# Seven half-size products for the first matrix of each MLP as well, in a float32 decoder trunk on one Trainium2 core

## The chip, the core and the metric

The kernel runs on one NeuronCore of a Trainium2 chip. The core has a matrix engine (TensorE, called PE below; its loads of stationary operands are listed apart as PEld), a vector engine (VectorE, DVE), a scalar engine (ScalarE, ACT), a general engine (GpSimd, POOL), and SyncE (SP), which here only starts transfers. Sixteen DMA engines move data between HBM and the on-chip memory SBUF; matrix products land in PSUM, which has eight banks of 512 float32 per partition. Each engine works through its own list of instructions in order and waits on semaphores that other engines raise.

The metric is the device time of one execution in microseconds (us), lower being better.

## What is computed

The input is 512 tokens of width 1024. A recurrent layer (Griffin RG-LRU) is followed by an MLP, then a differential-attention layer and a second MLP, and a final norm. The change touches the two MLPs and what lies around them:

```
def sq_relu_mlp(h, w1, w2):
    u = jax.nn.relu(h @ w1)
    return (u * u) @ w2

x = x + sq_relu_mlp(rmsnorm(x, mlp_norm[l]), mlp_w1[l], mlp_w2[l])   # for each of the two layers
```

`w1` is 1024 x 4096, `w2` is 4096 x 1024, and everything is float32. The kernel keeps float32 accuracy by writing each operand as hi + lo (hi is the operand rounded to the format fp32r, lo the rest) and adding three products: hi with hi, hi with lo, lo with hi.

## The kernel before, in words

All weights stream through the core as tiles of 128 x 1024 (512 KB). For every tile SP starts a load into one of two buffers (`w_raw`), ACT writes the rounded copy (`split_hi`, into one of four slots `w_hi`), DVE writes the rest (`split_lo`, into `w_lo`), and PE multiplies with both. ACT may write tile t's slot only when PE has finished tile t - 4 (the semaphore `tile_done`), so splits run at most three tiles ahead of PE.

Each MLP is cut into four groups of 1024 hidden columns. A group has two halves.

The first product ("up", `mlp_up`): eight tiles of `w1`, each 24 matmuls of 512 columns (8 chunks of the input x three products), all 512 tokens at once, results in banks 0 to 3. After each tile ACT takes the relu from PSUM and squares it, and ACT and DVE write the hi and lo parts of the activations.

The second product ("down", `mlp_down`) uses Winograd's form of Strassen's method over halves of the tokens, of the hidden columns and of the outputs: seven products of half size instead of eight. Its operands are sums of quarters. The activations' sums are made by DVE (`pair_sums`). The weights' sums are made in transit: POOL starts a DMA that adds a tile from HBM to what lies in a buffer (`accum_op=ALU.add` into `b11` or `b12`; "an add" below). An add may start when the split of the buffer's former content is done. A group has 14 tiles here, each 12 matmuls of 512 columns, 8 adds, 4 loads into `b11` and `b12` and 12 loads into `w_raw`. DVE adds the finished products to `y` (`add_product`), and PE waits for that (`y_read`) two products later.

The order of the work on every engine is written out by hand: the functions `mlp_up` and `mlp_down` stand once under each engine, each with its own order, and an engine that waits holds up all that stands behind it.

The new code has one function `mlp` on ACT and on DVE that counts tiles s = 0 to 27 of a group (0 to 13 up, 14 to 27 down). In the text that follows tile s means this count.

## Time and profile before

| | |
|---|---|
| median of 3 runs | 1066.42 us (1066.36 to 1066.42) |
| the profiled execution, and its span | 1066.65 us, 1065.0 us |
| PE busy | 1051.8 us, 99% of the span |
| DVE busy | 697.8 us, 66% |
| ACT busy | 583.0 us, 55% |
| POOL busy | 91.3 us, 9% |
| moved by DMA | 136.80 MB, 128 GB/s on average |
| the eight MLP groups | 81.6 us each |

A row of a group of instructions names the line, the engine, what is written and read, the shapes and the count, then busy time and the mean of one in ns, then the idle time of the engine just before them and what ended it. "PE 99%" does not say that PE works at its peak: the ends of matmuls are modelled, and consecutive ones overlap in the records. The distance from start to start tells the pace.

### The profile page before, as it was taken

The page shows a single profiled execution, that of the slowest core. Times are in us where ns is not written, and L with a number is a line of the kernel's source. Part 1 is how long each engine was busy: PE and PEld are TensorE (multiplying, and loading weights), DVE is VectorE, ACT ScalarE, POOL GpSimd, SP SyncE. Part 2 cuts the span into 40 slices and gives each one's busy share as a digit, 9 for nine tenths or more (in the row PEclk, how much of TensorE's full clock was granted, in tenths as well). Part 3 has the DMA queues.
Part 4 walks back from the last instruction along what each step waited for, and adds up shares of the span by engine and source line. Part 5 has one row for each costly group of instructions (what it writes and reads, how often), then busy time and mean ns, then how long its engine had stood idle before and what let it go on. Part 6 is the DMA issues. An engine that isn't in the chain of part 4 may idle for free.

```text
span 1065.0 us, 12738 instructions
## 1 busy us (share of the span) xinstructions
PE 1051.8 (99%) x4752; PEld 848.1 (80%) x4752; DVE 697.8 (66%) x1149; ACT 583.0 (55%) x948; POOL 91.3 (9%) x105
## 2 busy tenths in 40 slices
PE   9999999999999999999999999999999999999996
PEld 6777888888888888888877777778888888888884
DVE  7888865665665575579656666565475675565666
ACT  6699845536535535545435656555543643643654
POOL 1000041100100100100000000031100010010012
PEclk9999999999999999999999999999999999999998
DMA  7222237665665575542311111136467468367372
GB/s 263 80 79 93 80 125 198 103 210 157 103 195 163 102 194 179 99 119 89 130 60 60 60 61 40 60 104 193 99 134 224 115 122 238 101 136 231 105 158 79
DMA packets 38940, 136.80 MB, mean 128 GB/s; under 512 B 4448, under 2 KB 4576, under 8 KB 38752
## 3 DMA queue, kind: packets, MB, share of 16 engines
q1 hardware_dynamic: 29232, 101.20, 28.1%
q0 software_dynamic: 9216, 33.56, 18.8%
q10 hardware_dynamic: 432, 1.24, 0.3%
q8 instruction: 38, 0.62, 0.2%
q14 instruction: 22, 0.18, 0.1%
HBM read 133.89 MB, written 2.10 MB: 128 GB/s over the span
## 4 chain that ended last, share of the span: by engine, by line
PE 95%; DVE 2%; DMA 1%; ACT 1%; issue 0%; SPq 0%; DVEq 0%; ACTq 0%
PE ps L1646 55%; PE ps L1774 28%; PE ps L1832 4%; PE ps L1891 2%; PE ps L1917 2%; PE ps L1700 1%; PE ps L1906 1%; DMA x<-x_t 0%; DVE w_lo L996 0%; DVE acc L1025 0%; DMA w_raw<-weights 0%; PE ps L1758 0%; PE ps L1929 0%; PE ps L1766 0%; DVE value L1344 0%
## 5 line engine op out<-in xcount | busy, mean ns | idle before, releaser
L1646 PE MATMUL ps<-h_hi,w_hi 128*128 128x512 f32 x704 | 281.7, 400 | 1.0 <-DVE w_lo L1014 0.6
L1646 PE MATMUL ps<-h_hi,w_lo 128*128 128x512 f32 x704 | 275.1, 391 | 0.0
L1646 PE MATMUL ps<-h_lo,w_hi 128*128 128x512 f32 x704 | 274.9, 391 | 0.0
L538 ACT ACTIVATE w_hi<-w_raw 128x1024 fp32r<-128x1024 f32 x150 | 158.6, 1057 | 192.1 <-DMA w_raw<-weights 92.0
L996 DVE TENSOR_TENSOR w_lo<-w_raw,w_hi 128x1024 fp32r<-128x1024 f32 x150 | 183.8, 1238 | 56.8 <-ACT w_hi L538 56.4
L1774 PE MATMUL ps<-w_hi,a_hi 128*128 128x512 f32 x448 | 174.4, 389 | 0.0
L1774 PE MATMUL ps<-w_lo,a_hi 128*128 128x512 f32 x448 | 174.3, 389 | 0.0
L1774 PE MATMUL ps<-w_hi,a_lo 128*128 128x512 f32 x448 | 174.3, 389 | 0.0
L1646 PEld LDWEIGHTS ps<-h_hi,w_hi 128*128 128x128 f32 x704 | 132.6, 188 | 32.8 <-DVE w_lo L1014 3.0
L1646 PEld LDWEIGHTS ps<-h_lo,w_hi 128*128 128x128 f32 x704 | 132.9, 189 | 28.0 <-issue 1.9
L1646 PEld LDWEIGHTS ps<-h_hi,w_lo 128*128 128x128 f32 x704 | 132.6, 188 | 28.2
L802 ACT ACTIVATE w_hi<-b 128x1024 fp32r<-128x1024 f32 x80 | 84.4, 1056 | 90.7 <-PE ps L1774 53.9
L1312 DVE TENSOR_TENSOR w_lo<-b,w_hi 128x1024 fp32r<-128x1024 f32 x80 | 97.7, 1238 | 41.6 <-ACT w_hi L802 41.6
L1344 DVE SCALAR_TENSOR_TENSOR value<-ps,scale,value 128x512 f32<-128x512 f32 x104 | 73.4, 747 | 63.1 <-PE ps L1774 63.0
L502 POOL DMA_DIRECT2D b<-weights x64 | 54.8, 857 | 541.2 <-DVE w_lo L1312 371.3
L1774 PEld LDWEIGHTS ps<-w_lo,a_hi 128*128 128x128 f32 x448 | 84.1, 188 | 17.6
L1774 PEld LDWEIGHTS ps<-w_hi,a_hi 128*128 128x128 f32 x448 | 84.1, 188 | 17.5 <-DVE w_lo L1312 0.2
L1774 PEld LDWEIGHTS ps<-w_hi,a_lo 128*128 128x128 f32 x448 | 84.1, 188 | 17.3
L760 ACT ACTIVATE work<-ps 128x512 f32<-128x512 f32 x64 | 37.9, 593 | 86.1 <-PE ps L1646 86.0
L1285 DVE TENSOR_TENSOR a_lo<-work,a_hi 128x256 fp32r<-128x256 f32 x64 | 35.5, 555 | 39.4 <-ACT a_hi L769 39.3
L1646 PE MATMUL ps<-u_hi,w_hi 128*128 128x512 f32 x128 | 51.7, 404 | 0.0
L1646 PE MATMUL ps<-u_hi,w_lo 128*128 128x512 f32 x128 | 50.0, 391 | 0.0
(179 smaller groups left out, 1234.6 us busy)
## 6 DMA issues: line engine op xcount, KB each, us to landing
w_raw<-weights SPq DMA_DIRECT2D x150, 512.0 KB, 3.5
b<-weights POOLq DMA_DIRECT2D x64, 512.0 KB, 5.4
b<-weights SPq DMA_DIRECT2D x32, 512.0 KB, 5.7
x<-x_t SPq DMA_DIRECT2D x8, 256.0 KB, 6.2
y_t<-value SPq DMA_DIRECT2D x8, 256.0 KB, 2.3
w_raw<-weights SPq DMA_DIRECT2D x4, 256.0 KB, 5.1
gw<-gate_weights ACTq DMA_DIRECT2D x1, 1024.0 KB, 6.0
gain_rows<-final_gain SPq DMA_DIRECT2D x1, 512.0 KB, 6.5
```

What stands on the lines that cost most here:

```text
L502: nc.gpsimd.dma_start(to[:, half, :], weights[stored_tile(layer, g, place + half)], accum_op=ALU.add).then_inc(sum_in[name][half], 16)
L538: nc.scalar.activation(w_hi[:, t % RING, :], w_raw[:, r % RAWS, :], ACT.Copy).then_inc(whi_done, 1)
L760: nc.scalar.activation(work[:, m % 2, :], ps[:, m % RING, :], ACT.Relu).then_inc(bank_read, 1)
L802: nc.scalar.activation(w_hi[:, t % RING, :], QUARTERS[q][:, half, :], ACT.Copy).then_inc(whi_done, 1)
L996: nc.vector.tensor_tensor(w_lo[:, t % RING, :], w_raw[:, r % RAWS, :], w_hi[:, t % RING, :], ALU.subtract).then_inc(wlo_done, 1)
L1285: nc.vector.tensor_tensor(a_lo[:, j, first:end, :].rearrange("p o s -> p (o s)"), src, a_hi[:, j, first:end, :].rearrange("p o s -> p (o s)"),
L1312: nc.vector.tensor_tensor(w_lo[:, t % RING, :], QUARTERS[q][:, p % 2, :], w_hi[:, t % RING, :], ALU.subtract).then_inc(wlo_done, 1)
L1344: return nc.vector.scalar_tensor_tensor(out=to, in0=bank, scalar=scale2[:, half, tok:tok + 1], in1=to, op0=ALU.mult, op1=ALU.add)
L1646: ins = nc.tensor.matmul(ps[:, bank, :], w[:, slot, ws], o[:, k, :], start=(k == 0 and n == 0), stop=(k == NCH - 1 and n == 2))
L1774: ins = nc.tensor.matmul(ps[:, bank, :], a[:, j, op, ts], w[:, slot, ws], start=first and a is a_hi and w is w_hi, stop=end and w is w_lo, ...
L1832: ins = nc.tensor.matmul(ps[:, 4 * half + tok, :], o[:, k, ts], w[:, t % RING, cs], start=(i == 0 and n == 0), stop=(i == NCH - 1 and n == 2))
L1891: ins = nc.tensor.matmul(ps[:, BANK_SCORES + 2 * (j % 2) + c, 0:n], kq[rows, h % 2, 1, qb * P:(qb + 1) * P], kq[rows, h % 2, 0, 0:n], star ...
```

## The change

The first product of each MLP group is computed with seven products of halves as well, over halves of the input width, of the hidden columns and of the tokens. Its 14 tiles have 24 matmuls of 256 columns each. The operands made from x are prepared once per layer as halves and sums (`x_hi`, `x_lo`, seven of them), in `residual_step`. The weights' sums of both products come through two pairs of buffers, `q1` and `q2`, by a list (`SOURCES`) that says, per product, which buffer is read after how many loads and adds; `None` is a tile straight from `w_raw`. The three partial results that several outputs share are copied out of PSUM by ACT (`copied`) and added by DVE (`up_sum`). The activations' operands (`a_hi`, `a_lo`) now live in four slots and are made one product ahead of their use instead of all before the down product. The on-chip memory is laid out as one region with different tenants by stage.

```diff
+UP = ((H11, 0, True), (T1, 1, True), (T2, 0, False), (H21, 2, True), (T3, 0, False), (H22, 1, False),
+      (T4, 0, False))
...
-PER = NCH + 2 * NPROD
+PER = 4 * NPROD
...
+SOURCES = (("q2", 0, 0), ("q1", 0, 1), ("q1", 0, 2), None, ("q2", 0, 1), ("q1", 0, 3), None,
+           ("q1", 1, 3), ("q1", 1, 4), ("q1", 1, 5), None, ("q2", 1, 2), None, ("q1", 1, 6))
...
+            def load_group(layer, g):
...
+                load_quarter(layer, g, "q2", A11, down_tile(layer, g - 1, 8) if g else None)
+                if g:
+                    two(r, A12)
+                    load_quarter(layer, g, "q1", A21, down_tile(layer, g - 1, 12))
...
+            def add_first(layer, g):
+                add_quarter(layer, g, "q1", A22, loaded=0)
+
+            def add_others(layer, g):
+                for n in ((2, 0) if g == 0 else (0, 2)):
+                    if n:
+                        add_quarter(layer, g, "q1", A11, split=up_tile(layer, g, 2))
+                    else:
+                        add_quarter(layer, g, "q2", A21, split=up_tile(layer, g, 0))
+                add_quarter(layer, g, "q1", A12, split=up_tile(layer, g, 4))
+                add_quarter(layer, g, "q2", B22, loaded=1)
+                add_quarter(layer, g, "q1", B12, split=down_tile(layer, g, 0))
+                add_quarter(layer, g, "q1", B22, split=down_tile(layer, g, 2))
+                add_quarter(layer, g, "q1", B21, split=down_tile(layer, g, 4))
...
+            add_first(1, 0)
             accumulate(N_M1)
...
+            add_others(1, 0)
```

On ACT (`activated(…, 3)` reads banks 0 and 1, where the last up product ends):

```diff
+            def activated(layer, g, n):
+                group = layer * GROUPS + g
+                src, to, sign = ((r11[:, :], r11[:, :], 1.0), (r22[:, :], r22[:, :], -1.0),
+                                 (r12[:, :], r12[:, :], 1.0), (up_banks(0), r21, -1.0))[n]
+                if n < 3:
+                    act.wait_ge(up_added, 3 * group + n + 1)
+                else:
+                    act.wait_ge(tile_done, down_tile(layer, g, 0))
...
+                ins = nc.scalar.activation(to, src, ACT.Relu, scale=sign).then_inc(relu_done, 1)
+                act.wait_ge(relu_done, 4 * group + n + 1)
+                nc.scalar.activation(to, to, ACT.Square).then_inc(squared, 1)
...
+            def mlp(layer, g, between=None):
+
+                for s in range(PER):
+                    if s in (2, 4, 6):
+                        copied(layer, g, s // 2 - 1)
+                    if s == 14:
+                        activated(layer, g, 3)
+                        act_hi(layer, g, 1)
+                    if s or g:
+                        split_hi(up_tile(layer, g, s + RING - 1))
...
+                    if s in (8, 10, 12):
+                        activated(layer, g, s // 2 - 4)
+                    for i, at in enumerate((9, 14, 15, 17, 17, 19, 21)):
+                        if s == at and i != 1:
+                            act_hi(layer, g, i)
```

On DVE:

```diff
+            def up_sum(layer, g, n):
+
+                i, to, pair = ((3, r11, 2), (4, r22, 0), (5, r12, 1))[n]
+                group = layer * GROUPS + g
+                dve.wait_ge(tile_done, up_tile(layer, g, 2 * i + 1) + 1)
+                dve.wait_ge(up_copied, 3 * group + n + 1)
...
+                nc.vector.tensor_tensor(to[:, :], to[:, :], banks, ALU.add).then_inc(up_added, 1)
...
+            def mlp(layer, g, after=None):
...
+                for s in range(PER):
+                    i = s // 2 - NPROD - 1
+                    if s in (8, 10, 12):
+                        up_sum(layer, g, s // 2 - 4)
+                    if s == 16:
+                        act_sum(layer, g, 3)
...
+                    if s >= 16 and s % 2 == 0:
+                        add_product(layer, g, i)
+                    if s == 18:
+                        act_lo(layer, g, 4)
+                    if s < PER - 2 or not last:
+                        split_lo(up_tile(layer, g, s + RING - 1))
...
+                    if s == 10:
+                        act_lo(layer, g, 0)
+                    elif s == 13:
+                        act_sum(layer, g, 1)
+                    elif s == 14:
+                        act_lo(layer, g, 1)
+                        act_sum(layer, g, 2)
+                    elif s == 15:
+                        act_lo(layer, g, 2)
+                    elif s == 16:
+                        act_lo(layer, g, 3)
+                    elif s == 17:
+                        act_sum(layer, g, 4)
```

On PE, where the down product also waits for the operand of each product (`o_act`) and not for the pairs of chunks:

```diff
             def mlp_up(layer, g):
-                for m in range(NCH):
...
+                for i, (op, pair, fresh) in enumerate(UP):
...
+                    for half in range(2):
+                        t = up_tile(layer, g, 2 * i + half)
+                        pe.wait_ge(wlo_done, t + 1)
+                        for jj in range(2):
+                            j = 2 * half + jj
...
+                            for f in range(4):
+                                ws = slice(jj * S + f * P, jj * S + (f + 1) * P)
+                                to = ps[:, BANKS_UP[pair][f // 2], f % 2 * HALF:(f % 2 + 1) * HALF]
+                                for n, (w, o) in enumerate(((w_hi, x_hi), (w_hi, x_lo), (w_lo, x_hi))):
+
+                                    ins = nc.tensor.matmul(to, w[:, t % RING, ws], o[:, op, j, :],
...
+                            pe.wait_ge(olo_done, o_act(layer, g, i) + 1)
...
```

The first place is ACT where the up product of a group ends and the down product begins. Before, the last rows of the activations stand among splits of `b11` (names as in the code; `ps` is PSUM):

```order
L802 ACTIVATE w_hi<-b11 128x1024 [waits tile_done,t1_in1]
L760 ACTIVATE work<-ps 128x512 [waits tile_done]
L765 ACTIVATE work<-work 128x512 [waits olo_done,bank_read]
L772 ACTIVATE a_hi<-work 128x512 [waits sq_u_done]
L780 ACTIVATE a_hi<-a_sum 128x1024 [waits a_sum_done]
L802 ACTIVATE w_hi<-b11 128x1024 [waits tile_done,t2_in0]
```

Now, from the split of tile 15 to the split of tile 18 (the rows of `w_hi<-q1` are the splits of tiles 15, 16, 17 and 18):

```order
L613 ACTIVATE w_hi<-q1 128x1024 [waits tile_done,q1_in1]
L863 ACTIVATE r12<-r12 128x1024 [waits up_added]
L865 ACTIVATE r12<-r12 128x1024 [waits relu_done]
L613 ACTIVATE w_hi<-q1 128x1024 [waits tile_done,q1_sum_in0,q1_in0]
L863 ACTIVATE work<-ps 128x1024 [waits olo_done,tile_done]
L865 ACTIVATE work<-work 128x1024 [waits relu_done]
L883 ACTIVATE a_hi<-work 128x1024 [waits tile_done,a_sum_done]
L613 ACTIVATE w_hi<-q1 128x1024 [waits tile_done,q1_sum_in1,q1_in1]
L613 ACTIVATE w_hi<-q1 128x1024 [waits tile_done,q1_sum_in0,q1_in0]
```

Three rows of 1024 elements (relu from PSUM, square, the hi part of the down product's second operand) have come to stand between the splits of tiles 16 and 17.

The second place is DVE over the same stretch. Before:

```order
L1312 TENSOR_TENSOR w_lo<-b11,w_hi 128x1024 [waits whi_done] x2
L1295 TENSOR_TENSOR a_sum<-work 128x256 [waits olo_done,sq_u_done]
L1296 TENSOR_TENSOR a_sum<-work 128x256
L1298 SCALAR_TENSOR_TENSOR a_sum<-a_sum,work 128x256 [waits dve_own]
L1301 SCALAR_TENSOR_TENSOR a_sum<-work,a_sum 128x256 [waits dve_own]
L1285 TENSOR_TENSOR a_lo<-work,a_hi 128x512 [waits ohi_done]
L1312 TENSOR_TENSOR w_lo<-b11,w_hi 128x1024 [waits whi_done]
L1285 TENSOR_TENSOR a_lo<-a_sum,a_hi 128x1024 [waits ohi_done]
L1344 SCALAR_TENSOR_TENSOR value<-ps,scale2,value 128x512 [waits y_read,tile_done]
```

Now, from the splits of tiles 15 and 16 (the row with x2) to the reading of the first down product (`value` is y):

```order
L1109 TENSOR_TENSOR w_lo<-q1,w_hi 128x1024 [waits whi_done] x2
L1436 TENSOR_TENSOR work<-r22,r12 128x1024 [waits olo_done,squared]
L1109 TENSOR_TENSOR w_lo<-q1,w_hi 128x1024 [waits whi_done]
L1454 TENSOR_TENSOR a_lo<-work,a_hi 128x1024 [waits ohi_done]
L1445 SCALAR_TENSOR_TENSOR work<-work,r11 128x1024 [waits olo_done]
L1109 TENSOR_TENSOR w_lo<-q1,w_hi 128x1024 [waits whi_done]
L1454 TENSOR_TENSOR a_lo<-work,a_hi 128x1024 [waits ohi_done]
L1445 SCALAR_TENSOR_TENSOR work<-work 128x1024 [waits olo_done,squared]
L1465 SCALAR_TENSOR_TENSOR value<-ps,scale2,value 128x512 [waits y_read,tile_done]
```

The lo parts of the down product's operands stand between its weight splits and its sums now, each behind the split of a later tile. The second operand's sum and its lo part wait for the splits of tiles 16 and 17 to be through.

The third place is POOL, whose list is nearly all adds. Before, one group:

```order
L502 DMA b12<-weights 128x1024 [waits b12_in0]
L502 DMA b12<-weights 128x1024 [waits b12_in1]
L502 DMA b11<-weights 128x1024 [waits wlo_done] x6
```

Now one group, from its first add (the x6 at the end are the adds to tiles 16 to 19 and 26, 27):

```order
L539 DMA q1<-weights 128x1024 [waits q1_in0]
L539 DMA q1<-weights 128x1024 [waits q1_in1]
L539 DMA q2<-weights 128x1024 [waits wlo_done] x2
L539 DMA q1<-weights 128x1024 [waits wlo_done] x4
L539 DMA q2<-weights 128x1024 [waits q2_in0]
L539 DMA q2<-weights 128x1024 [waits q2_in1]
L539 DMA q1<-weights 128x1024 [waits wlo_done] x6
```

A group has 16 adds instead of 8, and the first six stand at its start: two on `q1`, two on `q2`, two on `q1` again.

## Rows read from the trace of the kernel before

**Rows 1.** The page: busy times, the chain that ended last, DMA queues.

```profile
PE 1051.8 (99%) x4752; PEld 848.1 (80%) x4752; DVE 697.8 (66%) x1149; ACT 583.0 (55%) x948; POOL 91.3 (9%) x105
...
q1 hardware_dynamic: 29232, 101.20, 28.1%
q0 software_dynamic: 9216, 33.56, 18.8%
...
PE 95%; DVE 2%; DMA 1%; ACT 1%; issue 0%; SPq 0%; DVEq 0%; ACTq 0%
```

**Rows 2.** Windows over group 1 of layer 0: up, down, whole.

```profile
core 0: us, PE busy (x) PEld busy (x) DVE busy (x) ACT busy (x) POOL busy (x), PEclk, DMA share, GB/s
253.70:297.20 43.50, 43.50 (x194) 36.02 (x193) 26.61 (x36) 24.53 (x32) 5.12 (x6) 1.00 0.58 113
297.20:335.30 38.10, 38.10 (x170) 31.55 (x169) 22.90 (x28) 15.73 (x18) 1.71 (x2) 1.00 0.65 202
253.70:335.30 81.60, 81.60 (x362) 67.57 (x361) 49.50 (x64) 40.26 (x50) 6.83 (x8) 1.00 0.61 155
```

**Rows 3.** PE in order of time: start us, us, what.

```profile
264.44 0.39 PE L1646 MATMUL ps<-h_hi,w_hi 128*128 128x512 f32 x1
...
266.02 0.39 PE L1646 MATMUL ps<-h_lo,w_hi 128*128 128x512 f32 x1
```

**Rows 4.** PE in order of time where fewer than 512 columns stream.

```profile
165.56 0.94 PE L1684 MATMUL ps<-ones,acc 128*128 128x1 f32 x8
...
654.83 0.28 PE L1917 MATMUL ps<-value,prob_t 128*128 128x128 f32 x1
...
658.61 0.83 PE L1917 MATMUL ps<-value,prob_t 128*128 128x128 f32 x6
```

**Rows 5.** The page's costliest groups: weight loads, splits, the relu.

```profile
L538 ACT ACTIVATE w_hi<-w_raw 128x1024 fp32r<-128x1024 f32 x150 | 158.6, 1057 | 192.1 <-DMA w_raw<-weights 92.0
...
L1646 PEld LDWEIGHTS ps<-h_hi,w_hi 128*128 128x128 f32 x704 | 132.6, 188 | 32.8 <-DVE w_lo L1014 3.0
...
L760 ACT ACTIVATE work<-ps 128x512 f32<-128x512 f32 x64 | 37.9, 593 | 86.1 <-PE ps L1646 86.0
```

**Rows 6.** ACT in order of time, with a wait for an add.

```profile
203.37 1.06 ACT L780 ACTIVATE a_hi<-a_sum 128x1024 fp32r<-128x1024 f32 x1 [1.08 <-DVE a_sum L1301]
204.34 1.04 ACT L802 ACTIVATE w_hi<-b 128x1024 fp32r<-128x1024 f32 x1
207.33 1.06 ACT L802 ACTIVATE w_hi<-b 128x1024 fp32r<-128x1024 f32 x1 [1.95 <-DMA b<-weights]
```

**Rows 7.** DVE in order of time.

```profile
205.42 1.23 DVE L1312 TENSOR_TENSOR w_lo<-b,w_hi 128x1024 fp32r<-128x1024 f32 x1 [1.47 <-ACT w_hi L802]
206.56 1.22 DVE L1285 TENSOR_TENSOR a_lo<-a_sum,a_hi 128x1024 fp32r<-128x1024 f32 x1
207.69 1.40 DVE L1343 TENSOR_SCALAR value<-ps,scale 128x512 f32<-128x512 f32 x2
```

**Rows 8.** POOL in order of time: two adds, and a step of the accumulation.

```profile
151.78 1.85 POOL L479 TENSOR_TENSOR acc<-acc,work 128x512 f32<-128x512 f32 x1 [3.58 <-ACT work L551]
...
202.03 0.85 POOL L502 DMA_DIRECT2D b<-weights  x1 [3.05 <-DVE w_lo L1312]
206.94 0.86 POOL L502 DMA_DIRECT2D b<-weights  x1 [4.06 <-DVE w_lo L1312]
```

**Rows 9.** DMA, window 1016.3:1025 (40 slices of 0.22 us): adds alone.

```profile
DMA  0000000971869999999997957949599999990000
...
q0 software_dynamic: 288, 1.05, 68.8%
```

**Rows 10.** DMA, window 233:245.4 (12.4 us): adds and loads together.

```profile
q1 hardware_dynamic: 620, 2.24, 51.6%
q0 software_dynamic: 288, 1.05, 47.9%
...
b<-weights POOLq DMA_DIRECT2D x1, 512.0 KB, 9.4
```

**Rows 11.** The page's DMA issues: KB each, median us from issue to landing.

```profile
w_raw<-weights SPq DMA_DIRECT2D x150, 512.0 KB, 3.5
b<-weights POOLq DMA_DIRECT2D x64, 512.0 KB, 5.4
b<-weights SPq DMA_DIRECT2D x32, 512.0 KB, 5.7
```

More of the change, by code:

```diff
@@ L36 @@
 T_OUT = len(IN_ORDER)
-A11, A12, A22, S1, S2, S3, S4 = range(7)
 NOP = 7
@@ L77 @@
 B_MLP0 = T_MLP0
-B_KV = B_MLP0 + NCH * GROUPS
+B_KV = B_MLP0
 B_V = B_KV + NCH
@@ L493, in _ @@
-            own.step(nc.gpsimd.affine_select(out=bias[:, :], in_=bias[:, :], compare_op=ALU.is_ge,
-                                             fill=MASKED, base=S - P, pattern=[[-1, S]],
-                                             channel_multiplier=1))
-            own.wait()
-            nc.gpsimd.tensor_scalar(bias[:, :], bias[:, :], SLOPE_0, 0.0, ALU.mult,
-                                    ALU.add).then_inc(consts_done, 1)
-            def add_weights(layer, g):
-                def add(name, half, to, place):
-                    nc.gpsimd.dma_start(to[:, half, :], weights[stored_tile(layer, g, place + half)],
-                                        accum_op=ALU.add).then_inc(sum_in[name][half], 16)
-                for half in range(2):
-                    pool.wait_ge(quarter_in["b12"][half], quarter_loads(layer, g))
-                    add("t3", half, b12, NCH)
-                for name, product, place in (("t1", 0, R_PER + 2), ("t2", 1, NCH), ("t4", 2, NCH + 2)):
-                    for half in range(2):
-                        pool.wait_ge(wlo_done, down_tile(layer, g, 2 * product + half) + 1)
-                        add(name, half, b11, place)
@@ L514, in _, with add_quarter @@
-            for g in range(GROUPS):
-                add_weights(0, g)
+            def add_quarter(layer, g, q, place, split=None, loaded=None):
+                for half in range(2):
+                    if split is None:
+                        pool.wait_ge(quarter_in[q][half], quarter_loads(layer, g, loaded))
+                    else:
+                        pool.wait_ge(wlo_done, split + half + 1)
+                    nc.gpsimd.dma_start(QUARTERS[q][:, half, :], weights[stored_tile(layer, g, place + half)],
+                                        accum_op=ALU.add).then_inc(sum_in[q][half], 16)
@@ L805, in mlp_down @@
-            def mlp_down(layer, g, between=()):
-                for p in range(2 * NPROD):
-                    if p + RING < 2 * NPROD:
-                        product_hi(layer, g, p + RING)
-                    else:
-                        split_hi(down_tile(layer, g, p + RING))
-                    for step in between:
-                        step(p)
+                    nc.scalar.activation(raw[:, m, :, :].rearrange("p n s -> p (n s)"), x[:, m, :], ACT.Copy,
+                                         scale=col(gains[0], gains[1] + m)).then_inc(x_raw_done, 1)
@@ new lines, in residual_step @@
+                    own.wait()
+                    own.step(nc.vector.scalar_tensor_tensor(out=sums[:, 1, :], in0=sums[:, 0, :], scalar=-1.0,
+                                                            in1=raw[:, m, 1, :], op0=ALU.mult,
+                                                            op1=ALU.subtract))
+                    own.step(nc.vector.tensor_tensor(sums[:, 2, :], raw[:, m, 1, :], raw[:, m - 1, 1, :],
+                                                     ALU.subtract))
+                    own.wait()
@@ L1768, in turn_y, with product_passes @@
                 ins.then_inc(turned, 1)
-            def product_passes(bank, slot, op, half, jj, n, first, end, goes_on):
+            def product_passes(bank, slot, a_slot, half, jj, n, first, end, goes_on):
                 j = 2 * half + jj
```

628 lines of the change are left out of this document (357 added, 271 removed).

## The prediction, made before the changed kernel ran

> **What bounds the kernel now.** I read the page first: PE is busy for 1051.8 of 1065.0 us and the chain that ended last lies on PE for 95%; nothing else reaches 3% [rows 1]. The windows over one MLP group come next, since the change lies there. A group takes 81.6 us, 43.5 up and 38.1 down, with PE busy throughout, DVE for 49.5, ACT for 40.3 and the DMA engines for 0.61 of it [rows 2]. PE's rows in order of time give its pace: seven starts in 1.58 us, 0.226 us per matmul of 512 columns [rows 3], or 43.5 us / 192 = 0.2267. So work taken from PE is gained in full, as long as the other engines and the transfers keep up with a faster PE. Whether they do is the question.
>
> **What goes from PE.** A group's up product has 8 x 24 = 192 matmuls of 512 columns and will have 14 x 24 = 336 of 256. The trace has no fp32r matmul of 256 columns. From below: a pair of weight load and matmul with 1 column takes (0.94 - 0.25) / 7 = 0.10 us, with 128 columns (0.83 - 0.28) / 5 = 0.11 us [rows 4]. From above: the 0.2267 of 512 columns, if the width doesn't matter, which would make the up product 76 us. I take half of 0.2267, 0.1133 us, since it lies beside the 0.11 row. If the 13 ns by which 0.2267 exceeds 512 columns at 2.4 GHz (granted clock 1.00 [rows 2]) are a cost of each matmul, it is 0.120. At 0.1133 a tile takes 2.72 us, as one of the down product does, and a group 28 x 2.72 = 76.2 us: 5.4 less than before, 43.5 in all eight. A weight load's record lasts 0.188 us [rows 5], longer than that; but pairs follow each other faster than such a record lasts [rows 4], so I don't let it bound the pace.
>
> The Trainium skill (TensorE: Matmul & The Clock Gate, Part 3, "What overlaps and what doesn't") says that a weight load overlaps with running matmuls only if its row group differs. By that a load would be paid beside every matmul, and the page's formula puts it at 128 / 1.2 = 107 ns. The trace disagrees: 0.226 us for 512 columns leaves 13 ns beside the streaming.
>
> **What the others get.** Per group, in rows of 1024 elements. ACT: 28 splits, 3 copies from PSUM, 8 relu and square, 7 hi parts: 46 x 1.06 = 48.7 us [rows 5, 6] (a row of 512 from PSUM takes 0.59, so PSUM is no dearer). DVE: 28 splits, 3 sums of products, 4 sums and 7 lo parts of activations at 1.22, and 7 x 1.40 for y: 61 us [rows 7]. DMA: 16 adds and 16 loads. An add alone: two adds, the second issued while the first ran, stream from slice 8 to slice 36 of 40, 29 x 0.2175 = 6.3 us, 3.15 each [rows 9]; the page gives the same, 18.8% of 1065 us / 64 = 3.13 [rows 1]. A load: 28.1% of 1065 / 193 = 1.55. Together 50 + 25 = 75 of 76.2 us. Two adds and 4.3 loads fill 12.4 us [rows 10], so they hardly overlap. Everything still fits on average; no engine has slack left for an order that makes it wait.
>
> **Stall B, tile 16.** The wait that the change adds on PE is for the lo part of each down product's operand, one product ahead, and behind it stands the whole rest of PE's list. Count from the end of tile 9. The links [rows 6 to 8]: a waiting engine starts 0.04 us after what it waits for (0.19 after PE's next matmul starts), rows on one engine that don't need each other start 0.97 (ACT) and 1.14 (DVE) apart, POOL starts 0.29 after DVE (205.42 + 1.23 to 206.94), and ACT may read an add 5.30 after POOL started it (202.03 to 207.33). DVE's sum of product 4 ends at 1.4, relu 2.5, square 3.6, and only then ACT splits tile 14: 4.6, DVE 5.85, add issued 6.15, landed for tile 16 at 11.45. ACT waits there, with the last relu behind it. Relu starts 12.4, square 13.5, hi part 14.45, split of tile 17 15.4 to 16.5, DVE's split 17.7, and the lo part of the second operand 18.9. PE wants it at tile 16, 6 x 2.72 = 16.3. Stall 2.6 us, of which 1.3 would remain without any lateness of the add.
>
> **Stall C, products 2 and 3 of down.** From PE's restart DVE has a sum, split, lo part, sum and the reading of product 0: 6.1 us, and PE waits for that read after 5.44; the next read is at 12.05 against 10.9. Together 1.2 us. Afterwards DVE does 4.8 us of work per 5.44, so its backlog only melts: the split of tile 26 ends 25.1 us after the restart, 8.7 before the next group, where the tiles alone would allow 11.2.
>
> **Stall D, tiles 4 and 5.** That split frees `q1`. Counted from the next group's start: load issued -8.7, landed -5.15 (3.5, rows 11), add issued -5.1, streaming from 1.6 later until -0.1. Behind it in the same queue stand the add of the other half, the two of `q2`, and then the two that tiles 4 and 5 need. At 3.15 each the fifth ends at 12.5, split on ACT and DVE 2.6 later, 15.1, against 4 x 2.72 = 10.9 on PE: 4.2 us. Tile 5 is 3.15 - 2.72 = 0.4 later still. D = 4.6.
>
> **Group 0 of each layer** has its buffers filled early, but POOL does `accumulate` first. The last square comes about 5.7 us after the group's start (x added 0.7, five ACT rows behind it), the last step takes 1.85 [rows 8], the add is issued at 7.9, readable 13.2, split 15.5: 4.6, and 0.4 again. D is 5.0.
>
> **The sum.** Groups 1 to 3: 76.2 + 2.6 + 1.2 + 4.6 = 84.6, 3.0 more than 81.6, six times 18. Groups 0: 85.0, twice 3.4. Together +24.8 us. The operands of x (about 3.4 us of ACT and 4.0 of DVE per chunk of x, by the rows) fit under the 5.4 us that PE spends on a tile there, so they cost nothing; the transposes and the tail stay. The profiled execution took 1066.65 against the median of 1066.42, so no correction: 1066.4 + 24.8 = 1091. At 0.120 per matmul a group has 2.2 more work, but B and D shrink by 0.7 each: about +1 per group, 1098.
>
> **Rivals.** The adds are quick (faster). If they streamed and landed like plain loads (1.55 and 3.5 us), D would be gone (tile 4 split by 6.6), B would be 1.3 and C 1.2: 78.7 per group, 1066.4 - 8 x 2.9 = 1043. If only D fell away and the rest stayed, 80.0 per group, 1054. The group breaks even where D is 1.6, at 2.5 us per add. For it: some slices are only half full while two adds stream [rows 9]; against it: 3.15 comes out of two views. If nothing stalls, 1066.4 - 43.5 = 1023.
>
> The Trainium skill (DMA: Bandwidth & Descriptors, "Anatomy of one DMA — SWDGE (gpsimd) path") fits a GpSimd transfer by 2.0 us + bytes / 436e3, 3.2 us for 512 KB. The median add here took 5.4 [rows 11]; by the page's figure this rival would hold.
>
> Adds and loads in each other's way (slower still). With loads about, an add landed only after 9.4 us [rows 10]. If the six adds at the group's start take 3.7 each, D is 5 x 3.7 - 11.1 = 7.4 and B grows by the same lateness of 0.6: 88 per group, 1117.
>
> A matmul of 256 columns as slow as the weight load's record, 0.188: up 63.2 us, group 101.3, 1066.4 + 8 x 19.7 = 1224. Only the records' length speaks for it.
>
> **Chances.** The forecast, all three stalls near their size (1076 to 1104): 50%. Quick adds, wholly or in D alone (1040 to 1060): 23%; no stall worth the name (about 1023): 4%. Crowded DMA (1104 to 1130): 20%. Slow matmuls: 3%. Predicted 1091; its own range is 1076 to 1104, and with the neighbours 1050 to 1118. Less than 0.2% (2.1 us) can't be told from no change; stalls of 5.4 us per group would land there. Faster 0.26, same 0.04, slower 0.70.
>
> **What the new profile would show.** PE no longer 99% busy but about 93%. Matmuls of 256 columns start 0.113 apart. PE idle in each group in three places: before tile 4, released by DVE's split of a `q1` tile, before tile 16, released by the lo part (L1454), and twice by the reading of y (L1465). In the DMA row the first 20 us of a group full with adds, six in a row. I am wrong if PE is gap-free, if the adds of one burst end less than 2.5 us apart, or if the 256-column matmuls start 0.12 or more apart and the stalls vanish behind them.

## The result: 1135.9 us against 1066.4, and the profile after

The changed kernel takes 1135.89 us (median of 4 runs, 1133.7 to 1145.5), the kernel before 1066.42 (1066.36 to 1067.13): ratio 1.067, 95% interval 1.061 to 1.073. It is 69.5 us slower where I forecast 24.8, and lies outside the range of 1050 to 1118. The profiled execution of it took 1137.5 us. All times here are medians of the fast runs; one of the four runs of `order` below was a slow one and is left out of its median.

The page of the changed kernel, against [rows 1]. PE is busy for about as long as before (1056.9 us against 1051.8) in a span that is 70 us longer, the adds (q0) take 33.0% of the DMA engines instead of 18.8%, and the chain that ended last, as far as the page follows it (a third of the span), runs through DMA, PE and DVE in near-equal parts instead of lying on PE for 95%.

```profile
PE 1056.9 (93%) x5904; PEld 903.5 (80%) x5904; DVE 784.5 (69%) x1125; ACT 648.9 (57%) x940; POOL 147.3 (13%) x169
...
PEclk9999998999999998999999999998999999999998
...
q0 software_dynamic: 18432, 67.12, 33.0%
q1 hardware_dynamic: 29232, 101.20, 25.8%
...
DMA 10%; PE 9%; DVE 8%; ACT 3%; issue 2%; POOL 0%; ACTq 0%; DVEq 0%
...
L1921 PE MATMUL ps<-x_hi,w_hi 128*128 128x256 f32 x896 | 262.6, 293 | 33.9 <-DVE w_lo L1109 21.2
```

Windows of the changed kernel over group 1 of layer 0, up and down, the counterpart of [rows 2]:

```profile
core 0: us, PE busy (x) PEld busy (x) DVE busy (x) ACT busy (x) POOL busy (x), PEclk, DMA share, GB/s
250.70:294.66 43.96, 40.54 (x338) 40.35 (x336) 22.92 (x20) 24.46 (x25) 7.10 (x9) 1.00 0.93 219
294.66:336.53 41.87, 38.89 (x170) 31.31 (x169) 35.70 (x36) 22.04 (x22) 6.34 (x8) 1.00 0.73 172
```

The up half costs 44.0 us: PE works for 40.5 and waits for 3.4, with the DMA engines busy for 0.93 of it. So the half-size products save 3 us of work, and the waits take them back. The same view over groups 0, 2 and 0 of layer 1:

```profile
153.94:250.70 96.76, 85.82 (x513) 78.02 (x512) 67.45 (x74) 53.10 (x58) 23.66 (x26) 0.93 0.71 169
...
336.53:424.44 87.91, 82.04 (x506) 74.47 (x504) 58.87 (x56) 46.60 (x46) 14.11 (x17) 0.96 0.81 192
758.25:860.52 102.27, 89.33 (x544) 81.32 (x545) 68.64 (x75) 58.03 (x67) 20.52 (x21) 0.92 0.67 161
```

I had forecast 84.6 for a group and 85.0 for a group 0. The six groups 1 to 3 take 85.8 to 90.0 (mean 87.9), and groups 0 take 96.8 and 102.3. By the starts of their tiles, the 9.5 us by which groups 1 to 3 exceed the bare pace (78.4, see **widths**) are 3.6 before tile 4, 2.7 before tile 16, 0.5 at the reading of y, and 2.6 in tiles 4, 5 and 16 themselves, which PE runs in part at half clock. Tile 4 of group 2, at a granted clock of 0.62 and 4.46 us long instead of 2.88:

```profile
351.96:356.42 4.46, 4.46 (x25) 4.46 (x26) 2.94 (x3) 3.85 (x4) 1.70 (x2) 0.62 0.64 110
```

The granted clock is below 1.00 in most of the groups; before it was 1.00.

How the wait before tile 4 comes about in group 1, in order of time, from POOL, ACT, DVE and PE of the changed kernel:

```profile
245.99 0.88 POOL L539 DMA_DIRECT2D q<-weights  x1 [17.61 <-DMA q<-weights]
248.39 2.61 POOL L539 DMA_DIRECT2D q<-weights  x3 [1.52 <-DMA q<-weights]
255.47 0.84 POOL L539 DMA_DIRECT2D q<-weights  x1 [4.46 <-DVE w_lo L1109]
...
252.85 1.06 ACT L613 ACTIVATE w_hi<-q 128x1024 fp32r<-128x1024 f32 x1 [6.27 <-DMA q<-weights]
255.34 1.06 ACT L613 ACTIVATE w_hi<-q 128x1024 fp32r<-128x1024 f32 x1 [1.43 <-DMA q<-weights]
263.34 1.06 ACT L613 ACTIVATE w_hi<-q 128x1024 fp32r<-128x1024 f32 x1 [6.94 <-DMA q<-weights]
...
264.43 1.23 DVE L1109 TENSOR_TENSOR w_lo<-q,w_hi 128x1024 fp32r<-128x1024 f32 x1 [5.45 <-ACT w_hi L613]
...
265.80 0.36 PE L1921 MATMUL ps<-x_hi,w_hi 128*128 128x256 f32 x1 [3.42 <-DVE w_lo L1109]
```

The add for tile 4 is issued at 255.47, behind two for `q2`, and is readable 7.9 us later. PE waits 3.4. That is stall D, forecast at 4.6.

By their landings in the trace, the six adds of this burst are 2.5, 2.5, 2.5, 3.0 and 2.4 us apart, not 3.15 as in my working. The first landed 2.1 us after the group's start, where I had it streamed by -0.1. The two errors cancel: I had the fifth end at 12.5, and it landed at 12.6. So the place and cause of stall D were forecast, and its size in part by luck.

### The profile page after: what moved, and what is told of

Same layout as the page of the kernel before. It is cut to its first block and busy times, and to the rows that moved or that the text cites. A ratio compares the mean times of both kernels' runs of the same rounds, so it can differ in the third digit from the quotient of the medians.

```text
span 1135.5 us, 15159 instructions
## 1 busy us (share of the span) xinstructions
PE 1056.9 (93%) x5904; PEld 903.5 (80%) x5904; DVE 784.5 (69%) x1125; ACT 648.9 (57%) x940; POOL 147.3 (13%) x169
## 5 line engine op out<-in xcount | busy, mean ns | idle before, releaser
L1109 DVE TENSOR_TENSOR w_lo<-q,w_hi 128x1024 fp32r<-128x1024 f32 x160 | 198.5, 1242 | 196.0 <-ACT w_hi L613 195.8
L613 ACT ACTIVATE w_hi<-q 128x1024 fp32r<-128x1024 f32 x160 | 168.8, 1055 | 251.2 <-DMA q<-weights 119.1
L1921 PE MATMUL ps<-x_hi,w_hi 128*128 128x256 f32 x896 | 262.6, 293 | 33.9 <-DVE w_lo L1109 21.2
L1921 PE MATMUL ps<-x_lo,w_hi 128*128 128x256 f32 x896 | 260.6, 291 | 0.0
L1921 PE MATMUL ps<-x_hi,w_lo 128*128 128x256 f32 x896 | 260.4, 291 | 0.0
L539 POOL DMA_DIRECT2D q<-weights x128 | 109.8, 933 | 922.8 <-DMA q<-weights 608.3
L1921 PEld LDWEIGHTS ps<-x_hi,w_hi 128*128 128x128 f32 x896 | 179.5, 200 | 36.6 <-ACT r L851 26.5
L1921 PEld LDWEIGHTS ps<-x_lo,w_hi 128*128 128x128 f32 x896 | 179.5, 200 | 0.3
L1921 PEld LDWEIGHTS ps<-x_hi,w_lo 128*128 128x128 f32 x896 | 179.2, 200 | 0.0
L1793 PE MATMUL ps<-in_hi,w_hi 128*128 128x512 f32 x128 | 53.7, 420 | 2.0 <-DVE w_lo L1127 1.2
L883 ACT ACTIVATE a_hi<-r 128x1024 fp32r<-128x1024 f32 x24 | 25.2, 1050 | 29.1 <-DVE r L1440 29.1
```

Source lines behind the costliest of these rows:

```text
L539: nc.gpsimd.dma_start(QUARTERS[q][:, half, :], weights[stored_tile(layer, g, place + half)], accum_op=ALU.add).then_inc(sum_in[q][half], 16)
L613: nc.scalar.activation(w_hi[:, t % RING, :], src, ACT.Copy).then_inc(whi_done, 1)
L883: nc.scalar.activation(a_hi[:, k % SLOTS, :, :].rearrange("p n s -> p (n s)"), src, ACT.Copy).then_inc(ohi_done, 1)
L1109: nc.vector.tensor_tensor(w_lo[:, t % RING, :], src, w_hi[:, t % RING, :], ALU.subtract).then_inc(wlo_done, 1)
L1793: ins = nc.tensor.matmul(ps[:, bank, :], w[:, slot, ws], o[:, k, :], start=(k == 0 and n == 0), stop=(k == NCH - 1 and n == 2))
L1921: ins = nc.tensor.matmul(to, w[:, t % RING, ws], o[:, op, j, :], start=fresh and j == 0 and f % 2 == 0 and n == 0, stop=j == PAIRS - 1 and ...
```

## The experiments

Times are medians of 4 to 10 runs (`order`: three, `widths`: one); the kernel before ran beside them at 1066.1 to 1066.7. Group lengths and starts of tiles are from the profiled executions.

**widths**: the disputed costs by themselves.

```
WIDTHS = (512, 256, 384, 128, 256)
...
            def run(cols, n):
                for i in range(n):
                    ws = slice((i % 4) * P, (i % 4 + 1) * P)
                    ins = nc.tensor.matmul(ps[:, i % 8, 0:cols], w_hi[:, 0, ws], w_hi[:, 1, 0:cols],
                                           start=True, stop=True)
...
            for cols in WIDTHS:
                run(cols, 96).then_inc(pe_done, 1)
```

> This kernel computes nothing of the reference (it stores zeros): TensorE runs 96 fp32r matmuls back to back at each of 512, 256, 384, 128 columns, a new weight block each time, then four blocks of 96 at 256 columns with pauses of one to four ScalarE copies between them (about 1.3, 2.3, 3.4 and 4.4 us); then, with all else idle, the GpSimd queue carries six plain loads of 512 KB, six adds, and six adds beside eight loads of SyncE. Theory: 512 columns 0.2267 us apart, and the 13 ns beyond 512/2.4 are a cost of each matmul: 256 columns 0.120, 384 columns 0.173, 128 columns 0.067 or the 0.10 to 0.11 that short pairs took before. Rival (my forecast): the 13 ns go with the width, 256 columns 0.113, 384 0.170. Second rival: the pair of load and matmul has a floor, 128 columns no faster than 256. Pauses: if the clock answers to a pause alone, the matmuls behind one of the pauses are 0.21 apart instead of 0.12 for some microseconds; if it needs other engines' work too, none are. Adds: by my forecast 3.15 us apart, alone or with loads; by what the bursts of the changed kernel suggest 2.0 to 2.7 alone and more beside loads.

Windows over the blocks of 512, 256, 384 and 128 columns (length of the window, then PE's busy time and count):

```profile
33.00:54.70 21.70, 21.70 (x97) 17.97 (x96) 0.00 (x0) 0.00 (x0) 1.00 0.00 0
54.80:66.20 11.40, 11.40 (x97) 11.40 (x96) 0.00 (x0) 0.00 (x0) 1.00 0.01 1
66.30:82.80 16.50, 16.50 (x98) 16.50 (x97) 0.00 (x0) 0.00 (x0) 1.00 0.00 1
83.00:93.50 10.50, 10.50 (x97) 10.50 (x95) 0.00 (x0) 0.00 (x0) 1.00 0.01 2
```

Start to start within a block: 0.2267, 0.120, 0.1735 and 0.112 us. The 13 ns are a cost of each matmul, and below 256 columns a floor of 0.11 shows. A tile of the up product takes 24 x 0.120 = 2.88 us, not 2.72. By the Trainium skill (TensorE: Matmul & The Clock Gate, "LDWEIGHTS (loading the stationary operand)") a load of 128 columns takes an estimated 107 ns. As a floor for the pair of load and matmul that is near the 0.112 measured here; as a price on top of the streaming the run doesn't bear it out.

PE in order of time, the four blocks behind the pauses: start, length of the block of 96, and the pause ahead of it.

```profile
118.00 11.77 PE L262 MATMUL ps<-w_hi 128*128 128x256 f32 x96 [1.15 <-ACT pause L250]
132.00 13.26 PE L262 MATMUL ps<-w_hi 128*128 128x256 f32 x96 [2.23 <-ACT pause L250]
148.59 11.78 PE L262 MATMUL ps<-w_hi 128*128 128x256 f32 x96 [3.32 <-ACT pause L250]
164.77 14.42 PE L262 MATMUL ps<-w_hi 128*128 128x256 f32 x96 [4.41 <-ACT pause L250]
```

Behind the pauses of 2.23 and 4.41 us the blocks are 1.5 and 2.6 us longer: the granted clock was 0.50 (1.2 GHz) for 3.4 and 6.8 us. Behind those of 1.15 and 3.32 us it stayed at 1.00. So a pause of PE with nothing but ACT's copies in it can bring it down, though not each one of a given length does.

POOL in the same run: six plain loads, six adds, then six adds beside eight loads.

```profile
179.51 3.33 POOL L234 DMA_DIRECT2D q<-weights  x6 [177.82 <-PE ps L262]
191.04 5.30 POOL L232 DMA_DIRECT2D q<-weights  x6 [8.20 <-DMA q<-weights]
209.09 0.10 POOL L237 MEMSET mark<- 128x1 f32 x1 [12.75 <-DMA q<-weights]
```

The loads take 11.5 us in all, the adds 18.05. By the packets' ends the loads follow each other at 1.5 us, the adds alone at 2.5, and beside the loads at 3.8. The queue's share of the sixteen engines, adds alone (window of 18 us) and adds beside loads (29 us):

```profile
q0 software_dynamic: 864, 3.15, 91.0%
...
q0 software_dynamic: 864, 3.15, 54.9%
```

That is 2.73 and 2.65 us of all engines per add: an add isn't dearer beside loads. Beside them one load lands with each add, so the 3.8 fits an add's 2.5 and a load's 1.3 in turn. My 3.15 was the price of an add that starts a row. The packets of the first add here take 3.1, those of the later ones 2.65 (one 2.8); in the kernel before, whose share gave me 3.13 [rows 1], 43 of the 64 adds ran with next to no load beside them, and these took 3.2.

By the fit of the Trainium skill (DMA: Bandwidth & Descriptors, "Anatomy of one DMA — SWDGE (gpsimd) path") 512 KB take an estimated 3.2 us, completion included. The first plain load of this run took 3.2 from its issue to its last packet and 3.6 until it had landed, 0.4 more than the fit. The first add took 4.95 and 5.3, so for adds the fit is 2 us short.

**order**, **actorder** and **all**: the waits that I had named, taken away by order alone.

```
-                for n in ((2, 0) if g == 0 else (0, 2)):      # order: POOL, q1's second sum first
+                for n in (2, 0):
```

> The changed kernel, with q1's second sum issued ahead of q2's first in all groups (before, in groups 0 alone). Theory: the adds for tiles 4 and 5 wait in the queue behind q2's two; they are issued at 255.4 and land at 263.3 in group 1, 7.9 us, where an undisturbed one lands in 5.0. Without them ahead, tile 4 starts about 2.9 us earlier and the slow clock behind the stall (1.5 to 2 us lost) goes with it in part: 6 groups x 3 to 4.5 = 18 to 27 us faster than the changed kernel, about 1112. Rival: the eight microseconds are the add's own time beside loads; then tile 4 starts where it did, and the time stays within 3 us of 1135.

```
+                    if s == 13: act_hi(layer, g, 1)           # actorder: ACT, ahead of split_hi(16)
+                    if s == 13: act_sum(layer, g, 1); act_lo(layer, g, 1)   # DVE, ahead of split_lo(16)
```

> The changed kernel, with the second down operand (sum, hi part and lo part) made ahead of the split of tile 16 on ScalarE and VectorE instead of behind the last relu and the split of tile 17. Theory: the wait of tile 16 (2.3 to 4.0 us in each group, and the slow clock behind it, 1.5 us) is made of this order, so that 8 x 2.5 to 4 = 20 to 32 us go, less up to 1.2 per group where products 2 and 3 then wait for y: about 1110. Rival: the late add for tile 16 holds PE instead (half of the 2.6 as I reckoned): 8 x 1.3 = 10 us go, about 1125.

```
+            accumulate(N_M0, ahead=<the first of q1's two adds for tiles 4 and 5>)   # all: both, and this in groups 0
```

> Both reorderings together, and in groups 0 the first half of q1's second sum issued ahead of the last step of accumulate. Theory: what each takes away adds up, 18 to 27 and 20 to 32, and groups 0 lose 6 to 9 us each of their wait before tile 4, so 1135.5 less 50 to 75: 1060 to 1085. With no stall at all and 0.120 us per matmul it would be 1066.4 - 8 x 3.2 = 1041. Rival: the stalls move to the next late add (tiles 6 to 8, 12 to 16), so that less than half of it is gained: over 1095.

Measured: order 1128.1 (1122 to 1137), actorder 1137.8, all 1126.1. All three theories of size fell; of the rivals only that of all, over 1095, held. The 8 us of order are no larger than the spread of its runs, and actorder gained nothing. In order's profiled execution the wait before tile 4 is gone in groups 1 and 2 of layer 0, but tiles 15 and 16 with their waits, 7.9 and 9.4 us there in the changed kernel, take 11.2 and 11.0. In actorder nothing waits before tile 16, and tile 18 starts 43.4 us behind tile 4 in group 1, against 43.0 in the changed kernel. ACT, DVE and PE there:

```profile
303.82 1.06 ACT L613 ACTIVATE w_hi<-q 128x1024 fp32r<-128x1024 f32 x1 [3.60 <-DMA q<-weights]
304.79 1.05 ACT L883 ACTIVATE a_hi<-work 128x1024 fp32r<-128x1024 f32 x1
...
304.91 1.23 DVE L1110 TENSOR_TENSOR w_lo<-q,w_hi 128x1024 fp32r<-128x1024 f32 x1 [2.30 <-ACT w_hi L613]
306.06 1.22 DVE L1455 TENSOR_TENSOR a_lo<-work,a_hi 128x1024 fp32r<-128x1024 f32 x1
307.38 1.23 DVE L1446 SCALAR_TENSOR_TENSOR work<-work 128x1024 f32<-128x1024 f32 x1
308.53 1.40 DVE L1466 SCALAR_TENSOR_TENSOR value<-ps,scale,value 128x512 f32<-128x512 f32 x2
...
310.08 0.76 PE L1957 MATMUL ps<-w_hi,a_hi 128*128 128x512 f32 x1 [3.49 <-DVE value L1466]
```

The add for tile 18 is what is late now. The split waits for it, and behind the split stand the operand's parts and the reading of y, for which PE waits. A wait taken away by order alone comes back at the next late add.

**fill** and **fill2**: the clock. Matmuls that nobody needs stand where PE waits.

```
+                    if i == 2 and g:                  # fill2: ahead of all waits of tile 4
+                        pe.wait_ge(y_read, sums_read(layer, g - 1, NPROD - 1))
+                        filler(4, FILL_D)             # 16 matmuls of 512 columns into bank 4
...
+                    if i == 1 and (layer, g) != (0, GROUPS - 1):   # ahead of tile 16
+                        pe.wait_ge(up_added, 3 * group + 3)
+                        filler(2, FILL_B)         # 11 matmuls
```

> The changed kernel with idle time of TensorE filled: ahead of its wait for tile 4 in groups 1 to 3 stand 16 matmuls of 512 columns into a bank that nobody reads (3.6 us), ahead of that for tile 16 in all groups but layer 0's last 11 of them (2.5 us). Nothing else moves, so the weights come when they came. Theory: TensorE's clock falls to half (1.2 GHz) behind a stall of these lengths, at 1.7 us per fall of 3.4 us; 34 us in all in the MLPs, of which about 20 lie behind these two stalls. So the time falls by 15 to 22 us, to 1114 to 1120, though work is added, and the granted clock is 1.0 behind tiles 4 and 16 of the filled groups. Rival: what is lost behind a stall would be waited for anyway (the adds are late whatever the clock), then it stays within 5 us of 1135.

fill took 1164.8, far from both the theory and its rival. The fillers of tile 4 stood behind the wait for the copy of the first product, which is itself behind the late add on ACT, so they made the stall longer instead of filling it:

```profile
265.63 5.52 PE L1885 MATMUL ps<-x_hi 128*128 128x512 f32 x16 [3.75 <-ACT r L852]
```

> As the run fill, but the 16 matmuls stand ahead of the wait for the copy of the first up product too. In fill they stood behind it, and that copy (ScalarE, behind the split of tile 4 in its list) came only at the end of the stall, so the fillers lengthened it: tile 3 to tile 4 took 12.1 us instead of 6.5. Theory: the fall of the clock behind tile 4 costs 8 to 9 us over groups 1 to 3 of both layers and goes; behind tile 16 nothing is gained, since in fill TensorE ran tiles 16 to 18 at full clock and then waited 0.8 and 0.5 us for the reads of y that the slow clock had hidden. 1124 to 1130. Rival: late adds decide whatever the clock, 1133 to 1138.

fill2 took 1135.1 (1134.7 to 1138.8), the same as the changed kernel, though the clock's falls went: their loss within the MLPs is 34.1 us in the changed kernel and 13.7 in fill2. Windows over group 2 of fill2, to be read against 336.53:424.44 above: clock 1.00, and the same length.

```profile
337.69:425.47 87.78, 85.38 (x533) 76.68 (x531) 58.69 (x56) 46.51 (x46) 13.30 (x17) 1.00 0.84 191
```

The rival held: the adds decide when PE may go on, and a faster PE only waits longer at the next of them. In groups 1 to 3 the 2.6 us in tiles 4, 5 and 16 shrink to 0.3, and 0.6 more is waited before tile 4, 0.9 before tile 16 and 1.0 at the reading of y. The fillers themselves are a small part of this: in three of the six groups they end at 15.2 us after the group's start, half a microsecond behind the weights of tile 4.

**noadds** and **plain**: the adds left out, and replaced by plain loads on the same queue.

```
-                for half in range(2):                 # noadds: no add, and no split waits for one
+                for half in range(0):
...
-                                        accum_op=ALU.add).then_inc(...)     # plain
+                                        ).then_inc(...)
```

> The changed kernel without any of the 128 adds in the MLPs (each tile is split as its buffer was loaded; the output is of other weights). Order, splits, sums and loads stay. Theory: nearly all stalls come from adds that are late and from what stands behind them in ScalarE's and VectorE's order; without them a group takes 78.4 us (14 tiles of 2.88 and 14 of 2.72) plus about 1.3 at tile 16 and 1.2 at the reading of y, and groups 0 keep their wait for x's operands (3 to 5 us, with the clock's fall): 1066.4 - 25.4 + 8 x 1 to 2.5 + 2 x 5 = 1055 to 1071. Rival: ScalarE's and VectorE's own work binds beside the adds: over 1090.

> The changed kernel with each add replaced by a plain load of the same 512 KB on the same queue with the same waits (the weights are then not summed, the output differs). A load on that queue streams at 1.5 us and an add at 2.5 (run widths), everything else is as before. This is my rival of quick adds. Theory 1: the adds' bandwidth and the lateness of 1 us each in a burst of six is what holds tiles 4, 5, 16 and 18: most of the 69 us between noadds (1066.4) and the changed kernel go, 1070 to 1090. Theory 2: it is the serial path split, issue, landing, split, whose fixed part (some 3 us of queue and completion) stays: over 1110.

noadds 1066.4 (1065.2 to 1067.3), ratio to before 1.000 (0.999 to 1.001); plain 1088.4, ratio 1.021 (1.019 to 1.022). Windows over group 1, up and down of noadds, and the whole group of plain:

```profile
236.46:276.77 40.31, 40.31 (x337) 40.30 (x336) 23.03 (x21) 24.56 (x24) 0.00 (x0) 1.00 0.34 106
276.77:317.54 40.77, 38.94 (x170) 31.31 (x169) 35.76 (x37) 22.09 (x22) 0.00 (x0) 1.00 0.34 103
```

```profile
247.47:328.50 81.03, 79.21 (x506) 71.61 (x504) 58.68 (x56) 45.79 (x46) 8.43 (x16) 1.00 0.65 205
```

noadds lies where its theory had it (1055 to 1071), plain where its first had it (1070 to 1090). All 69 us between the changed kernel and the one before hang on the adds. In groups 1 to 3 plain is as fast as noadds, 81.0 and 81.1: the serial path (split, issue, landing, split) fits in time, and it is the extra microsecond that the DMA engines spend on each add that costs 6.8 us per group. Groups 0 stay long in plain (92.5 and 96.8, in noadds 81.9 and 89.3), so most of their loss has another cause: the places that the transfers have in POOL's list (g0 below).

**ring**: a shorter chain of adds in the down product, bought with two more loads per group.

```
-           ("q1", 1, 3), ("q1", 1, 4), ("q1", 1, 5), None,
+           None, ("q1", 1, 4), ("q1", 1, 5), None,
```

> As the run all, and the down product's first quarter also comes through the ring of w_raw (two more loads of 512 KB per group), so that q1's first sum for down is made from its load and not behind the split of tiles 14 and 15. Theory: in the down product three uses of q1 follow each other at 5.44 us on TensorE, while one step of add and split takes 5.3 + 2.6 = 8 us; that is what held tile 18 in actorder and all (3.7 to 5 us with the clock's fall). One step less removes most of it: 8 x 3 to 5 = 24 to 40 us below 1126, 1086 to 1102. Rival: ScalarE's and VectorE's lists are what is late, or the two loads more crowd the adds: within 5 us of 1126.

1168.9, 43 us slower than all. Four adds are now issued between 283.1 and 288.1, and the load for tile 14, issued at 285.7, is readable at 294.2, 8.5 us later. ACT in group 1:

```profile
294.25 1.06 ACT L617 ACTIVATE w_hi<-w_raw 128x1024 fp32r<-128x1024 f32 x1 [5.28 <-DMA w_raw<-weights]
```

The wait before tile 18, which the shorter chain was to remove, did not shrink: from tile 17 to tile 18 it is 8.4 us on average over the eight groups, against 7.9 in all. So my theory's number fell, and the rival's "within 5 us" too: the groups are 5 to 6 us longer with the two loads, and from 283.0 to 294.3, where they fall, the DMA engines are busy throughout. That the loads are dear because of this is inferred from the share alone, and what the shorter chain would bring without them is not shown.

**late** and **noadds_late**: the operands of product 2 and the reading of product 0 ahead of the split of tile 18, added to **all** and, with actorder's order, to **noadds**.

```
+                    if s == 15: act_hi(layer, g, 2)                       # ACT
+                    if s == 15: act_lo(layer, g, 2); act_sum(layer, g, 3); add_product(layer, g, 0)   # DVE
```

> As the run all, and the third down operand (hi and lo part) and the reading of product 0 now stand ahead of the split of tile 18 on ScalarE and VectorE. In actorder's trace that split waits for its add until 303.8, and a_hi, a_lo, the next sum and the reading of y stand behind it; TensorE gets y at 310.0 though product 0 was done near 298. Theory: tile 18 then starts behind its own weights, 4 us earlier in each group: 8 x 2 to 4 us below 1126, 1094 to 1110. Rival: the stall moves on to the next late add, 1120 to 1130.

> The run noadds with the orders of actorder and late. noadds showed every group of layer 0 and 1 at 81.1 us with 1.3 us before tile 16, 0.8 before tile 18 and 0.3 before tile 20 (2.6 and 1.2 forecast, 1.3 of it without late adds). Theory: these are made of the order of the rows alone and go here: 8 x 1.0 to 2.4 below 1066.4, 1047 to 1058, groups at 78.7 to 80. Rival: the work moved ahead of the splits makes these late in turn, 1064 or more.

late 1115.0 (1109.3 to 1116.9), 11 below all: less than the 16 to 32 expected, more than the rival's. noadds_late 1063.7 (1063.4 to 1064.3), only 2.7 below noadds, so its theory fell: groups take 80.8 instead of 81.1, with 1.8 us before tile 18 in place of 1.3 and 0.8 before tiles 16 and 18. So without late adds the rows of ACT and DVE at the start of the down product are a limit of their own, in both of the orders tried.

**g0** and **best**: POOL's order in groups 0. In the changed kernel, from POOL, ACT, DVE and PE at the end of layer 0's output projection:

```profile
137.88 1.03 POOL L539 DMA_DIRECT2D q<-weights  x1 [131.62 <-DMA q<-weights]
139.17 0.86 POOL L539 DMA_DIRECT2D q<-weights  x1 [0.26 <-DMA q<-weights]
139.72 0.93 POOL L527 COPY acc<-work 128x512 f32<-128x512 f32 x1
...
140.68 0.63 ACT L625 ACTIVATE work<-x 128x512 f32<-128x512 f32 x1 [5.58 <-POOL acc L527]
...
142.30 2.32 DVE L1109 TENSOR_TENSOR w_lo<-w_raw,w_hi 128x1024 fp32r<-128x1024 f32 x1 [6.00 <-ACT w_hi L613]
...
161.36 0.39 PE L1921 MATMUL ps<-x_hi,w_hi 128*128 128x256 f32 x1 [2.95 <-DVE x_lo L1400]
```

POOL waits for `q1`'s load with `accumulate` behind it. ACT's square waits 5.6 us for `accumulate`, and the splits and all operands of x wait behind the square. At the end of the chain are the last square and, behind the last step of `accumulate`, the adds for tiles 4 and 5:

```profile
165.86 0.61 ACT L625 ACTIVATE work<-x 128x512 f32<-128x512 f32 x1
...
168.49 3.52 POOL L539 DMA_DIRECT2D q<-weights  x4
```

```
-            add_first(0, 0); accumulate(N_M0)
+            accumulate(N_M0, <add_first ahead of step 4, one add for tile 4 ahead of step 7>)
```

> The changed kernel, with two places moved on POOL in groups 0 alone: the first adds to q1 stand behind four steps of accumulate instead of ahead of all, and the first of the two adds for tiles 4 and 5 ahead of its last step. Theory: in the changed kernel the first adds wait on POOL for their loads, accumulate stands behind them, ScalarE's square waits 5.6 us (5.3 in layer 1) for it, and with it all operands of x; that is what TensorE misses at tile 1 and what makes the adds for tiles 4 and 5 late. Both go: tile 1 loses 2.5 to 4 us, tile 3 to 4 another 3 to 6, in two groups: 11 to 20 us below 1135.9, 1116 to 1125. Rival: the loads and adds themselves hold the ring's load, and VectorE's rows per chunk of x are the limit (noadds kept 7.2 us at layer 1's tile 1): under 5 us gained.

> All reorderings together (late and g0). Theory: the gains add, 1115.0 less 8 to 18 us, 1097 to 1107, still slower than the kernel before, since adds at 2.5 us (3.8 beside loads) stay. Rival: late already had the half of it that stands ahead of accumulate's last step, so that under 5 us are left, over 1110.

g0 took 1124.3 (1118.9 to 1129.1), 11.6 below the changed kernel. Its groups 0 take 89.3 and 98.5, 7.5 and 3.8 less, together 11.3, about what the median gains (groups 1 to 3 are 0.7 longer each in this execution, the longest of its four); the wait at tile 1 is gone in layer 0. In layer 1 a wait at tile 1 stays, as it does without any add (7.2 us for the tile in noadds). best took 1103.8 (1094.3 to 1106.8), ratio to before 1.034 (1.029 to 1.038). That fits its theory (1097 to 1107). No version that computes the result beat the kernel before.

## Why the prediction was wrong, step by step

**The sign and the mechanism of groups 1 to 3 held.** Stall D stood where I put it, at 1.5 to 5.6 us against 4.6. Stall B was 2.3 to 4.0 us against 2.6; without late adds 1.3 of it remained, as forecast. Stall C was 0.8 and 0.3 us in noadds against 1.2. What late adds cost a group above its own order was 6.8 us against 4.6 + 1.3 = 5.9. The size of D owes something to luck, as said above: the adds of a burst end some 2.5 us apart, which is the edge of what I had named as a sign of being wrong, and the stall came all the same.

**Groups 0: "they cost nothing" was the step that failed.** I let the operands of x hide under PE's 5.4 us per tile and counted the last square at 5.7 us after the group's start. It came at 165.9, 12 us after it, and tile 4 started at 176.3, 22.4 us after it instead of 15.5. I had read that POOL does `accumulate` first, and not that the first two adds stand ahead of it and wait for a load there; ACT, DVE and PE are behind that. The two groups took 11.8 and 14.1 us more than forecast (the second less 3.2 for eight sets of transposes that the kernel before has there too), 26 of the 45 us by which the sum was short. g0 shows 11 of these to be POOL's order; noadds shows 5 in layer 1 (89.3 - 3.2 - 81.1) to be there without adds, and the pace below has 4. The other 5 are not told apart.

**The pace of 256 columns** was mis-sized: 0.120 and not 0.1133, 2.2 us per group. I had the reading that proved right as the alternative, and let it cost only 1 us per group, "B and D shrink by 0.7 each". D did so (4.6 forecast, 3.6 measured on average), B did not (2.7 against 2.6), since an add is issued when a split is done, and the splits follow PE. The pace is 6 x 2.2 = 13 us in groups 1 to 3. There a group took 3.3 more than forecast: 2.2 of pace and 2.6 in tiles run in part at half clock, less 1.6 by which the waits together were smaller than 8.4 (the parts leave 0.1 over). Six times 3.3 and the 26 of groups 0 are the 45 us.

**"Everything still fits on average"** was true and of no use. The DMA engines are busy for 0.83 of group 1, but for 0.93 of its up half. Of the rivals, crowded DMA came nearest in number, 88 us per group where 87.9 were measured, but that is luck. It set 3.7 us for each add of the burst at the group's start and 7.4 for D; in the six groups 1 to 3 these adds landed 2.4 to 3.2 us apart, once 4.4, and D was 3.6. Nor had it the groups 0. Quick adds had the right lever: with adds as quick as loads (plain) stall D is gone and a group takes 81.0 us, its 78.7 plus the 2.2 of the pace. The adds are just not quick.

**The clock** was not in my sum. It fell behind the stalls and lost 34 us by its own account, but in fill2 20 of these are gone and the time is the same: what the half clock takes would else be waited for.

The account, against the kernel before: PE's work -25.6 us (78.4 instead of 81.6 in eight groups); waits that the order makes without any late add, 2.7 in each of eight groups, 0.8 and 5 more in groups 0, +27; together about nothing, as noadds measured. The adds: +40.6 in groups 1 to 3 and +28 in groups 0, 69 in all. With plain loads in their place nothing of the 40.6 is left, and 18 of the 28. So in groups 1 to 3 it is the adds' slowness, and in groups 0 mostly what the waits in POOL's list hold up. How the 40.6 part between the adds' own 2.5 us and the loads that take turns with them is open.

## What to carry to other kernels

When work is taken from the bounding engine and the others are at nine tenths in some stage, look at that stage's share, not at the group's mean, and replace the suspected transfer by a plain one of the same size before anything is reordered: that one run told more than three reorderings. Before pricing a wait on an in-order engine, list what stands behind it there, POOL's DMA issues included. And don't count the clock's falls as a cost until a run has filled the gap without gaining.

## What the hardware showed that I had not expected

- A DMA that adds to SBUF streams 512 KB in 2.5 us where the same queue loads it in 1.5. Beside loads from another queue the adds land 3.8 apart, with one load to each; the engines' time per add stays 2.65.
- An fp32r matmul costs its columns at 2.4 GHz plus 13 ns at 256, 384 and 512 columns alike, and pairs of load and matmul come no closer than 0.112 us at 128 columns.
- The granted clock fell to 0.50 behind a pause of 2.23 us and did not behind one of 3.32 us, with the same work around both.
